# A hybrid encoder trunk on one core: setup with the modulation first, latent weights loaded raw ahead, two tiles kept on chip, and the first gate formed in the output stage

## The chip, the cores and the metric
The kernel runs on one core of a Trainium2 chip. The metric is the device time of one execution in microseconds (us). All matrix products of the model run on TensorE as three products of a high and a low part ("hi", "lo") in float32r, so that a weight or an activation is always split first: ScalarE copies the high part, VectorE or GpSimd subtracts it from the source to give the low part.

## The reference
Two layers over a sequence of 2048 tokens of width 1024. Each layer is `x + gate * RMSNorm(mixer(RMSNorm(x) * (1 + scale) + shift))`, where shift, scale and gate come from `silu(c) @ ada_w + ada_b`.
```
def _even_mixer(h, cos, sin, w_in, ...):
    rq, rk, rv, rg, cq, ckv, kr, mg = _split(h @ w_in, EV_SPLITS)
    # A: bidirectional retention on rq, rk (rope), rv, chunks of 128; * silu(rg)
    # B: latent attention: q from rmsnorm(cq) @ w_uq, k and v from rmsnorm(ckv) @ w_ukv,
    #    one rotary key kr shared by 4 heads, dense softmax; * silu(mg)
    return jnp.concatenate([ret_out, mla_out], axis=-1) @ w_out
```
The second layer's mixer (a convolution module) is not touched.

## The kernel before
The work is a row of stages. Each stage is one block with its own semaphores, in which the five engines run their own written-out queues; a stage starts when every engine has ended the one before. SP issues all loads and stores.

`setup` (L129) loads `ada_w` in eight slabs of 1024 KB and the first weight columns (`w1`, 1536 wide) in eight slabs of 768 KB, in turn. VectorE adds the slabs weighted by `silu(c)` into `acc` (L323, L326), with the rope angles (L266 to L279), the decay logarithms (L289 to L299) and exponents (L305 to L311) after the first sums. ScalarE makes `w_hi` (L205), GpSimd `w_lo` (L229). TensorE then turns `acc` into columns (L240) for `shift` and `gain`.

`project_retention` (L338) goes over 16 tiles of 128 tokens, last tile first. Per tile: norm (L454, L457), transpose (L606), modulation (L466), split (L472, L543), three projections `ps_qk`, `ps_v`, `ps_g` of 24 matmuls (L612 to L614), rope, the backward state. `h` and a pack of 2560 columns are stored for each tile (L417, L422). The gate row of the modulation is summed on the side (L578).

`project_mla` (L695) goes over the tiles forwards. Its weight pieces come through four staging slots in the two packs, four of them loaded ahead in the stage before; ScalarE and VectorE split them (L672, L680). TensorE forms the first gate (L1109, L1110), VectorE multiplies it by the post-norm weight (L1016), and only then the tiles begin: `ps_cq`, `ps_ckv`, the retention scores, `ps_mg`, and the up projections `ps_cq`, `ps_mg`, `ps_s` out of the latents (L1027 to L1029).

`attention` (L1118) loads the shared rotary key whole (L1285) and splits it in two forms `kr_same` and `kr_swap` of 2048 columns (L1344, L1462, L1466, L1468) before the first scores (L1484). `even_out` (L1552) splits the output weight in eight pieces, transposes mix tiles (L1757) and multiplies (L1779 to L1781); its residual step uses the first gate (L1734).


## Time and profile before
| what | value |
|---|---|
| time, median of 3 runs | 2511.83 us (2511.54 to 2513.14) |
| profiled execution, its own time | 2515.42 us |
| its span | 2513.6 us |
| TensorE busy | 2286.7 us, 91% |
| VectorE, ScalarE, GpSimd busy | 55%, 45%, 40% |
| mean granted clock of TensorE | 0.969 of full |

The span is the time from the first to the last instruction. Engines are named PE (TensorE), PEld (its weight loads), DVE (VectorE), ACT (ScalarE), POOL (GpSimd), SP (SyncE); a q after the name means its queue of DMA issues. [...] In brackets behind an instruction stands how long its engine sat idle before it and who released it.

### The profile page before, as it was taken

To read this page: it belongs to the slowest core of one execution; us is meant where nothing else is said; L and a number is where in the kernel's file an instruction comes from. 1 tells how busy PE (TensorE), PEld (TensorE's weight loads), DVE (VectorE), ACT (ScalarE), POOL (GpSimd) and SP (SyncE) were. 2 spreads that over 40 slices of the span, in tenths; PEclk is the share of its full clock that TensorE was granted. 3 is DMA by queue.
4 is the path that set the end of the run, shared out by engine and by line. 5 is a ranking of instruction groups with operands and counts; after the bars stand their busy time and mean duration, and the time that the engine had idled before them with its cause. 6 is when DMAs were issued, how large, how long until landed. Compare 5 with 4: busy or idle time off the path is not lost. (4 is left out here: it accounts for less than half of the span.)

```text
span 2513.6 us, 34469 instructions
## 1 busy us (share of the span) xinstructions
PE 2286.7 (91%) x11378; PEld 1898.7 (76%) x11378; DVE 1392.1 (55%) x2092; ACT 1132.4 (45%) x2090; POOL 1011.9 (40%) x741
## 2 busy tenths in 40 slices
PE   0799997999998699999999969997999999995998
PEld 0688885989887487787887758885878888874886
DVE  8233334434433577777777631114888889864332
ACT  2444443222222455555555535554455555553332
POOL 4222220222222423233233102333789998873443
PEclk9999998999999899999999979998999999997999
DMA  6234335334343533343342133321011112124553
GB/s 258 103 139 146 133 117 197 137 132 143 131 148 102 153 104 97 98 113 96 104 113 80 47 130 126 125 101 42 26 50 52 59 65 70 55 109 130 162 149 115
DMA packets 194607, 279.94 MB, mean 111 GB/s; under 512 B 10837, under 2 KB 139221, under 8 KB 189271
## 3 DMA queue, kind: packets, MB, share of 16 engines
q1 hardware_dynamic: 189910, 270.41, 33.4%
q10 hardware_dynamic: 4608, 8.39, 0.9%
q8 instruction: 51, 0.84, 0.1%
q14 instruction: 38, 0.30, 0.0%
HBM read 188.05 MB, written 90.70 MB: 111 GB/s over the span
## 5 line engine op out<-in xcount | busy, mean ns | idle before, releaser
L1957 POOL TENSOR_TENSOR conv_g<-conv_g,product 128x1024 f32<-128x1024 f32 x160 | 379.5, 2415 | 41.4 <-ACT product L1986 41.4
L2053 DVE SCALAR_TENSOR_TENSOR ps_conv<-u,cols,ps_conv 128x1024 f32<-128x1024 f32 x304 | 364.8, 1285 | 0.0
L2092 PE MATMUL ps_z<-ho_hi,wp_lo 128*128 128x512 f32 x768 | 302.6, 394 | 23.9 <-POOL wp_lo L1947 18.9
L2093 PE MATMUL ps_z<-h_left,wp_hi 128*128 128x512 f32 x768 | 301.7, 393 | 0.0
L2094 PE MATMUL ps_z<-ho_hi,wp_hi 128*128 128x512 f32 x768 | 301.4, 392 | 0.0
L1986 ACT ACTIVATE product<-u,cols 128x1024 f32<-128x1024 f32 x160 | 181.9, 1151 | 144.5 <-POOL conv_g L1957 139.1
L1315 ACT ACTIVATE pt_hi<-ps_pt 128x512 fp32r<-128x512 f32 x256 | 154.2, 603 | 200.3 <-PE ps_pt L1496 198.8
L1414 DVE TENSOR_TENSOR pt_lo<-ps_pt,pt_hi 128x512 fp32r<-128x512 f32 x256 | 176.0, 688 | 116.8 <-ACT pt_hi L1315 114.1
L1404 DVE TENSOR_REDUCE mx<-ps_s 128x1 f32<-128x512 f32 x256 | 173.4, 685 | 39.8 <-PE ps_s L1488 38.8
L2092 PEld LDWEIGHTS ps_z<-ho_hi,wp_lo 128*128 128x128 f32 x768 | 146.0, 190 | 56.2 <-POOL wp_lo L1947 19.7
L1308 ACT ACTIVATE probs<-ps_s,bias 128x512 f32<-128x512 f32 x256 | 174.0, 698 | 24.1 <-DVE bias L1410 16.5
L1360 POOL TENSOR_TENSOR v_lo<-v_st,v_hi 128x512 fp32r<-128x512 f32 x64 | 84.1, 1314 | 242.9 <-DVE v_hi L1390 242.9
L2094 PEld LDWEIGHTS ps_z<-ho_hi,wp_hi 128*128 128x128 f32 x768 | 145.9, 190 | 30.8
L2093 PEld LDWEIGHTS ps_z<-h_left,wp_hi 128*128 128x128 f32 x768 | 146.2, 190 | 30.2
L1496 PE MATMUL ps_pt<-const,probs 128*128 128x128 f32 x1024 | 154.2, 273 | 4.1 <-DVE pt_lo L1414 3.1
L1496 PEld LDWEIGHTS ps_pt<-const,probs 128*128 128x128 f32 x1024 | 125.5, 140 | 42.8 <-DVE pt_lo L1414 11.5
L1355 POOL TENSOR_TENSOR k_lo<-k_st,k_hi 128x512 fp32r<-128x512 f32 x64 | 85.8, 1353 | 169.7 <-ACT k_hi L1299 169.6
L1484 PE MATMUL ps_s<-k_hi,q_lo 128*128 128x512 f32 x256 | 114.5, 447 | 36.4 <-DVE kr_swap L1468 23.6
L1505 PE MATMUL ps_ot<-pt_hi,v_lo 128*128 128x512 f32 x256 | 111.2, 434 | 5.1 <-ACT o_t L1334 5.1
L2338 PE MATMUL ps_yo<-w_last_hi,mo_lo 128*128 128x512 f32 x256 | 103.3, 404 | 7.8 <-DVE mo_lo L2283 7.8
L1734 DVE SCALAR_TENSOR_TENSOR mod_acc<-ps_y,ry_e,gate 128x1024 f32<-128x1024 f32 x16 | 20.5, 1284 | 154.9 <-POOL ry_e L1707 154.9
L1779 PE MATMUL ps_y<-wo_hi,m_lo 128*128 128x512 f32 x256 | 103.2, 403 | 0.0
(341 smaller groups left out, 5668.7 us busy)
## 6 DMA issues: line engine op xcount, KB each, us to landing
scratch_ret_pack<-pack SPq DMA_DIRECT2D x16, 1280.0 KB, 5.4
pack<-scratch_ret_pack SPq DMA_DIRECT2D x16, 1280.0 KB, 6.7
k_st<-scratch_k_t SPq DMA_DIRECT2D x64, 256.0 KB, 3.5
v_st<-scratch_v SPq DMA_DIRECT2D x64, 256.0 KB, 3.7
ada<-in_ada_w_dram SPq DMA_DIRECT2D x16, 768.0 KB, 6.4
wp_raw<-in_od_w_in_dram SPq DMA_DIRECT2D x24, 512.0 KB, 3.9
ada<-in_ada_w_dram SPq DMA_DIRECT2D x8, 1024.0 KB, 6.3
xt<-in_x_dram SPq DMA_DIRECT2D x16, 512.0 KB, 6.2
```

The source lines that it names most:

```text
L1308: act.activation(probs[s][b][:, kb * BANK:(kb + 1) * BANK], ps_s[kb][:], ACT.Exp, bias=bias[b % 2][:], scale=SCALE, accum_out=sums[s][:, b ...
L1315: act.activation(pt_hi[kt % 4][:], ps_pt[kt % 2][:], ACT.Copy).then_inc(pthi_done, 1)
L1404: dve.tensor_reduce(mx[:, kb:kb + 1], ps_s[kb][:], AX.X, ALU.max).then_inc(max_done, 1)
L1414: dve.tensor_tensor(pt_lo[kt % 4][:], ps_pt[kt % 2][:], pt_hi[kt % 4][:].bitcast(F32), ALU.subtract).then_inc(ptlo_done, 1)
L1484: pe.matmul(dst, q_lo[s][:, q], k_hi[s][:, k], start=True, stop=False)
L1496: mm = pe.transpose(ps_pt[kt % 2][:, qb * P:(qb + 1) * P], probs[sl][qb][:, kt * P:(kt + 1) * P], ident)
L1957: pool.tensor_tensor(half(conv_g, h), half(conv_g, h), product[h][:], ALU.add).then_inc(added, 1)
L1986: act.activation(product[h][:], units(c, V_TAPS + i, h), ACT.Copy, scale=tap_w).then_inc(product_done, 1)
L2053: ins = dve.scalar_tensor_tensor(acc[h][:], units(c, k, h), w, acc[h][:], ALU.mult, ALU.add)
L2092: pe.matmul(dst, lo[:, k, :], h_hi[:, k, t], start=k == 0, stop=False)
L2093: pe.matmul(dst, hi[:, k, :], h_lo[:, k, t], start=False, stop=False)
L2094: mm = pe.matmul(dst, hi[:, k, :], h_hi[:, k, t], start=False, stop=k == KD - 1)
```

## The change
Five parts.

**Setup.** Only the two last tiles of x and `ada` are loaded at first, then `w1` raw into the place of `w_lo`, in three thirds of columns. The modulation sums are kept in PSUM (`acc_ps`), and their columns are summed after a transpose. The decay logarithms and exponents come first on VectorE. The first tile's norm and transposes, and the high part of the first weight third, are made here.
```
-            for k in range(KD + 1):
-                if k < KD:
-                    if k >= NW:
-                        sp.wait_ge(mod_sum, k - NW + 1)
-                    sp.dma_start(ada[:, k % NW, :], ada_view[k][:, 0:2 * D]).then_inc(ada_in[k % NW], 16)
-                if k > 0:
-                    n = k - 1
-                    if n >= NS:
-                        sp.wait_ge(lo_done, n - NS + 1)
-                    sp.dma_start(stage[:, n % NS, :], w_view[n][:, w_cols[0]:w_cols[1]]).then_inc(w_in[n % NS], 16)
-            for dst, src in ahead:
-                sp.dma_start(dst, src).then_inc(x_ahead, 16)
-            sp.wait_ge(x_ahead, 16 * len(ahead))
+            for i, src in enumerate(x_pieces):
+                sp.dma_start(xt[:, i, :], src).then_inc(x_ahead[i], 16)
+            for k in range(KD):
+                if k >= NW:
+                    sp.wait_ge(mod_sum, k - NW + 1)
+                sp.dma_start(ada[:, k % NW, :], ada_view[k][:, 0:2 * D]).then_inc(ada_in[k % NW], 16)
+            for j in range(3):
+                for k in range(KD // 2):
+                    sp.dma_start(w_raw[:, 2 * k:2 * k + 2, j * BANK:(j + 1) * BANK],
+                                 w_view[k][:, :, j * BANK:(j + 1) * BANK]).then_inc(w_in[j], 16)
+            sp.wait_ge(x_ahead[1], 16)
...
-            split_w(1)
-            act.wait_ge(v_step, 101)
-            act.activation(st.sin[:].rearrange("p t f -> p (t f)"), red[:, 0, :], ACT.Sin)
-            act.activation(st.cos[:].rearrange("p t f -> p (t f)"), red[:, 1, :], ACT.Sin).then_inc(a_step, 1)
-            act.wait_ge(v_step, 102)
+            act.wait_ge(v_step, 3)
             act.activation(tiny[:, 1, :], tiny[:, 0, :], ACT.Exp, scale=-1.0).then_inc(a_step, 1)
+            act.wait_ge(x_ahead[0], 16)
+            act.activation(sq, xt[:, 0, :], ACT.Square, accum_out=ssq[:]).then_inc(sq_done, 1)
+            act.wait_ge(rstd_done, 1)
+            act.activation(xn[:], xt[:, 0, :], ACT.Copy, scale=rstd[:]).then_inc(xn_done, 1)
...
+            act.wait_ge(w_in[0], 64)
+            for k in range(KD // 2):
+                at = slice(2 * k, 2 * k + 2), slice(0, BANK)
+                act.activation(w_hi[:, *at], w_raw[:, *at], ACT.Copy)
...
-            pool.memset(st.neg_half[:], -0.5)
-            for k in range(KD):
-                pool.wait_ge(hi_done, k + 1)
-                pool.tensor_tensor(w_lo[:, k, :], stage[:, k % NS, :], w_hi[:, k, :].bitcast(F32),
-                                   ALU.subtract).then_inc(lo_done, 1)
+            pool.memset(st.neg_half[:], -0.5).then_inc(ms_done, 1)
+            pool.wait_ge(sq_done, 1)
+            pool.tensor_scalar(ms[:], ssq[:], 1.0 / D, EPS, ALU.mult, ALU.add).then_inc(ms_done, 1)
+            pool.wait_ge(ms_done, 2)
+            pool.tensor_tensor(rstd[:], ms[:], st.neg_half[:, 0:1], ALU.pow).then_inc(rstd_done, 1)
...
+            pe.wait_ge(xn_done, 1)
+            for k in range(KD):
+                pe.transpose(ps_h[k // 4][:, (k % 4) * P:(k % 4 + 1) * P], xn[:, k * P:(k + 1) * P], ident)
             pe.wait_ge(mod_sum, KD)
             for m in range(2 * KD):
-                mm = pe.matmul(mod_ps[:, m:m + 1], acc[:, m * P:(m + 1) * P], ones[:, 0:1], start=True, stop=True)
-            mm.then_inc(mod_done, 1)
+                mm = pe.transpose(acc_ps[:, m * P:(m + 1) * P], acc[:, m * P:(m + 1) * P], ident)
+                if m % 4 == 3:
+                    mm.then_inc(mod_turned, 1)
...
                     dve.wait_ge(mod_sum, k)
-                    ins = dve.scalar_tensor_tensor(acc[:], ada[:, k % NW, :], st.silu_c[:, k:k + 1], acc[:], ALU.mult, ALU.add)
+                    if k == KD - 1:
+                        dve.wait_ge(sq_done, 1)
+                    ins = dve.scalar_tensor_tensor(acc if k == KD - 1 else acc_ps[:], ada[:, k % NW, :],
+                                                   st.silu_c[:, k:k + 1], acc_ps[:], ALU.mult, ALU.add)
                 ins.then_inc(mod_sum, 1)
...
-            dve.wait_ge(mod_done, 1)
+            for m in range(4):
+                dve.wait_ge(mod_turned, m + 1)
+                ins = dve.tensor_reduce(mods[:, 4 * m:4 * m + 4], acc_ps[:, m * BANK:(m + 1) * BANK].rearrange("p (a b) -> p a b", b=P),
+                                        AX.X, ALU.add)
+            step(ins)
```
**Retention stage.** The angles, sine and cosine move here, and so do the low parts of all weight thirds and the high parts of two. The latent columns of the next stage's weights (`first_raw`, 640 wide, all eight rows of blocks) are loaded raw once the waves are made. The last two tiles are not stored; their `h` and packs stay on chip.
```
             step(0, 0, 0)
+            sp.wait_ge(waves_done, 1)
+            for dst, src in ahead:
+                sp.dma_start(dst, src).then_inc(ahead_in, 16)
             step(1, 1, 0)
...
-                store(NT - 2 + s, s)
             sp.wait_ge(ahead_in, 16 * len(ahead))
             for s in range(2):
-                sp.wait_ge(h_stored[s], 16 * NT // 2)
-                sp.wait_ge(pack_stored[s], 16 * NT // 2)
+                sp.wait_ge(h_stored[s], 16 * (NT // 2 - 1))
+                sp.wait_ge(pack_stored[s], 16 * (NT // 2 - 1))
...
+            split_w(1)
             norm(1, 1, 0)
+            act.wait_ge(angles_done, 1)
+            act.activation(st.sin[:].rearrange("p t f -> p (t f)"), red[:, 0, :], ACT.Sin)
+            act.activation(st.cos[:].rearrange("p t f -> p (t f)"), red[:, 1, :], ACT.Sin).then_inc(waves_done, 1)
+            split_w(2)
             def step(t, s, pair):
                 turn_out(t + 1, 1 - s, pair + s)
...
+            pool.sem_inc(ms_ready, 1)
+            pool.sem_inc(rstd_ready, 1)
+            split_w(0)
+            split_w(1)
             rstds(1, 1)
+            split_w(2)
             for t in range(2):
                 rotate(t)
                 rstds(t + 2, t)
...
             dve.memset(back[:], 0.0).then_inc(back_copied, 1)
             dve.wait_ge(back_copied, 1)
+            split_w(0)
+            angles()
             split_lo(0, 0)
+            residues()
+            split_w(1)
+            split_w(2)
...
+                if isinstance(t, int) and t == 0:
+                    pe.wait_ge(wlo_done[0], 4)
...
+                if isinstance(t, int) and t == 0:
+                    pe.wait_ge(wlo_done[1], 4)
                 project(ps_v, s, BANK, v_done)
...
+                if isinstance(t, int) and t == 0:
+                    pe.wait_ge(wlo_done[2], 4)
                 project(ps_g, s, 2 * BANK, g_done)
```
**Second projection stage.** Tiles 0 and 1 use what lies on chip. Latent weights are split at once; the other columns and the up-projection weights are loaded raw into the place of their low parts and split by pieces, the latter inside tile 0. The gate is no longer formed here.
```
-            load_h(0)
-            sp.dma_start(gate_bias, st.rows[:, R_GATE:R_GATE + D]).then_inc(row_in, 16)
-            sp.dma_start(post, st.rows[:, R_POST:R_POST + D].broadcast_to([P, D])).then_inc(post_in, 16)
-            load_pieces(sp, pieces, stage, w_in_sem, wlo_done, AHEAD)
-            sp.wait_ge(wlo_done, NP)
-            load_pack(0, 0)
+            for k in range(KD // 2):
+                sp.dma_start(wi_raw[:, 2 * k:2 * k + 2, LORA:], tail_view[k][:, :, RET_COLS + LORA:RET_COLS + MLA_COLS])\
+                  .then_inc(tail_in[k], 16)
+            sp.dma_start(ukv_raw[:], ukv_view).then_inc(ukv_in, 16)
+            sp.dma_start(uq_raw[:], uq_view).then_inc(uq_in, 16)
...
+                if isinstance(t, int) and t == 0:
+                    split_up()
...
-                if not (isinstance(t, int) and t == NT - 1):
+                if not (isinstance(t, int) and t in (0, NT - 1)):
                     split_h(t + 1, 1 - s)
...
+            act.sem_inc(hi_ready, 2)
+            for k in range(KD):
+                act.activation(wi_hi[:, k, 0:LORA], first_raw[:, k, :], ACT.Copy).then_inc(lora_hi, 1)
+            for k in range(KD // 2):
+                act.wait_ge(tail_in[k], 16)
+                at = slice(2 * k, 2 * k + 2), slice(LORA, MLA_COLS)
+                act.activation(wi_hi[:, *at], wi_raw[:, *at], ACT.Copy).then_inc(tail_hi, 1)
...
+            for k in range(KD // 4):
+                at = slice(2 * k, 2 * k + 2), slice(MG, MLA_COLS)
+                pool.wait_ge(tail_hi, k + 1)
+                pool.tensor_tensor(wi_lo[:, *at], wi_raw[:, *at], wi_hi[:, *at].bitcast(F32), ALU.subtract).then_inc(mg_lo, 1)
...
-                hold(dve, st, pack_in[s], 16 * pair + 16)
+                if not (isinstance(t, int) and t < 2):
+                    hold(dve, st, pack_in[s], 16 * pair)
...
+                if isinstance(t, int) and t == 0:
+                    split_up()
                 hold(dve, st, chi_ready, t + 1)
...
+            dve.sem_inc(lo_ready, 2)
+            for k in range(KD):
+                dve.wait_ge(lora_hi, k + 1)
+                dve.tensor_tensor(wi_lo[:, k, 0:LORA], first_raw[:, k, :], wi_hi[:, k, 0:LORA].bitcast(F32),
+                                  ALU.subtract).then_inc(lora_lo, 1)
+            for k in range(KD // 2):
+                at = slice(2 * k, 2 * k + 2), slice(LORA, MG)
+                dve.wait_ge(tail_hi, k + 1)
+                dve.tensor_tensor(wi_lo[:, *at], wi_raw[:, *at], wi_hi[:, *at].bitcast(F32), ALU.subtract).then_inc(kr_lo, 1)
+            for k in range(KD // 4, KD // 2):
+                at = slice(2 * k, 2 * k + 2), slice(MG, MLA_COLS)
+                dve.tensor_tensor(wi_lo[:, *at], wi_raw[:, *at], wi_hi[:, *at].bitcast(F32), ALU.subtract).then_inc(mg_lo, 1)
...
+                first = isinstance(t, int) and t == 0
+                in_columns(ps_cq, s, 0, QR, cq_done, lora_lo if first else None)
                 pe.wait_ge(v_out, t)
+                if first:
+                    pe.wait_ge(kr_lo, KD // 2)
                 in_columns(ps_ckv, s, CKV, KVR + ROPE, ckv_done)
...
+                if first:
+                    pe.wait_ge(mg_lo, KD // 2)
                 in_columns(ps_mg, s, MG, H * DV, mg_done)
...
-                pe.wait_ge(wlo_done, NP)
+                if first:
+                    pe.wait_ge(up_lo, (KVR + QR) // P)
...
-            pe.wait_ge(row_in, 16)
-            for n in range(2):
-                c = slice(n * BANK, (n + 1) * BANK)
-                pe.matmul(gate_ps[n][:], ones, st.gate[0][:, c], start=True, stop=False)
-                mm = pe.matmul(gate_ps[n][:], ones[0:1, :], gate_bias[:, c], start=False, stop=True)
-            mm.then_inc(gate_step, 1)
-            pe.wait_ge(gate_step, 2)
-            pe.wait_ge(wlo_done, KD)
```
**Attention.** The rotary key is loaded by ScalarE's queue in parts of 512 and 1536 columns; the first query's low part is made by VectorE, not GpSimd.
```
 
-            for half in range(2):
-
-                sp.dma_start(probs[0][0][half * ROPE:(half + 1) * ROPE, :], st.kr_t).then_inc(kr_in, 16)
+            load_k(0, 0)
             load_q(0)
...
-            act.activation(kr_same[:], probs[0][0][:], ACT.Copy).then_inc(kr_hi, 1)
-            for q in range(QB):
+            for i, c in enumerate(KR_PARTS):
+                for half in range(2):
+                    r = slice(half * ROPE, (half + 1) * ROPE)
+                    act.dma_start(probs[0][0][r, c], st.kr_t[:, c]).then_inc(kr_in[i], 16)
+            for i, c in enumerate(KR_PARTS):
+                act.wait_ge(kr_in[i], 32)
+                act.activation(kr_same[:, c], probs[0][0][:, c], ACT.Copy).then_inc(kr_hi, 1)
+                act.activation(kr_swap[:, c], probs[0][0][:, c], ACT.Copy).then_inc(kr_hi, 1)
+                if i == 0:
+                    split_k(0, 0, 0)
+            for q in range(1, QB):
                 split_k(0, 0, q)
-            act.wait_ge(kr_ready, 2)
+            act.wait_ge(kr_ready, 4)
             over_groups(act, group)
...
-            split_q(0, 0)
+            pool.sem_inc(q_ready, 1)
...
 
-            dve.wait_ge(kr_in, 32)
-            dve.tensor_copy(kr_swap[:], probs[0][0][:]).then_inc(kr_hi, 1)
             split_q(0, 0)
-            dve.wait_ge(kr_hi, 2)
-
-            dve.tensor_tensor(kr_same[ROPE:P, :], probs[0][0][ROPE:P, :], kr_same[ROPE:P, :].bitcast(F32),
-                              ALU.subtract).then_inc(kr_ready, 1)
-            dve.tensor_tensor(kr_swap[0:ROPE, :], probs[0][0][0:ROPE, :], kr_swap[0:ROPE, :].bitcast(F32),
-                              ALU.subtract).then_inc(kr_ready, 1)
+            dve.wait_ge(qhi_done, 1)
+            dve.tensor_tensor(q_lo[0][:], q_st[:], q_hi[0][:].bitcast(F32), ALU.subtract).then_inc(qlo_first, 1)
+            for i, c in enumerate(KR_PARTS):
+                dve.wait_ge(kr_hi, 2 * i + 2)
+                dve.tensor_tensor(kr_same[ROPE:P, c], probs[0][0][ROPE:P, c], kr_same[ROPE:P, c].bitcast(F32),
+                                  ALU.subtract).then_inc(kr_ready, 1)
+                dve.tensor_tensor(kr_swap[0:ROPE, c], probs[0][0][0:ROPE, c], kr_swap[0:ROPE, c].bitcast(F32),
+                                  ALU.subtract).then_inc(kr_ready, 1)
             over_groups(dve, group)
 
         @block.tensor
...
+                if isinstance(n, int) and n == 0 and b == 0:
+                    pe.wait_ge(qlo_first, 1)
+                    pe.wait_ge(kr_ready, 2 if kb == 0 else 4)
```
**Output stage.** It forms the first gate before its first tile.
```
-            sp.dma_start(gate_bias[:], st.rows[:, R_GATE + D:R_GATE + 2 * D]).then_inc(row_in, 16)
+            sp.dma_start(gate_bias[:, 0], st.rows[:, R_GATE:R_GATE + D]).then_inc(row0_in, 16)
+            sp.dma_start(post[:], st.rows[:, R_POST:R_POST + D].broadcast_to([P, D])).then_inc(row0_in, 16)
...
+            dve.wait_ge(gate0_done, 1)
+            dve.wait_ge(row0_in, 32)
+            dve.tensor_tensor(st.gate[0][:], ps_y[1][:], post[:], ALU.mult).then_inc(gate0_ready, 1)
+            dve.wait_ge(gate0_ready, 1)
...
+                if isinstance(t, int) and t == 1:
+                    pe.wait_ge(gate0_ready, 1)
...
+            pe.wait_ge(row0_in, 32)
+            for n in range(2):
+                c = slice(n * BANK, (n + 1) * BANK)
+                pe.matmul(ps_y[1][:, c], ones, st.gate[0][:, c], start=True, stop=False)
+                mm = pe.matmul(ps_y[1][:, c], ones[0:1, :], gate_bias[:, 0, c], start=False, stop=True)
+            mm.then_inc(gate0_done, 1)
```

## Rows read from the trace of the kernel before
**Rows 1.** Waits of TensorE over the span: us in total, times, longest.
```profile
PE mod_ps L240 <- DVE acc L326: 60.5, 1, 60.5
PE ps_s L1484 <- DVE kr_swap L1468: 23.6, 1, 23.6
...
PE ps_m L1757 <- DVE wo_lo L680: 13.6, 1, 13.6
```
**Rows 2.** Timeline of the setup: start us, duration us, engine, line, operation.
```profile
11.66 0.69 DVE L266 TENSOR_TENSOR ang<-pos,table 128x512 f32<-128x512 f32 x1
...
15.42 3.42 POOL L229 TENSOR_TENSOR w_lo<-stage,w_hi 128x1536 fp32r<-128x1536 f32 x1 [14.58 <-ACT w_hi L205]
...
15.50 4.42 DVE L276 SCALAR_TENSOR_TENSOR red<-turns,red 128x1024 f32<-128x1024 f32 x1
...
25.68 2.35 DVE L326 SCALAR_TENSOR_TENSOR acc<-ada,silu_c,acc 128x2048 f32<-128x2048 f32 x1
...
28.29 0.17 DVE L289 TENSOR_SCALAR tiny<-tiny 128x8 f32<-128x8 f32 x1 [0.26 <-ACT tiny L215]
...
32.40 0.17 DVE L299 TENSOR_TENSOR lg<-turns,tiny 128x8 f32<-128x8 f32 x1
...
38.10 0.17 DVE L311 TENSOR_SCALAR expw<-lg 128x8 f32<-128x8 f32 x1
...
74.27 1.98 SPq L425 DMA_DIRECT2D pack<-in_ev_w_in_dram  x4
```
**Rows 3.** The page's groups: VectorE's convolution steps.
```profile
L2053 DVE SCALAR_TENSOR_TENSOR ps_conv<-u,cols,ps_conv 128x1024 f32<-128x1024 f32 x304 | 364.8, 1285 | 0.0
```
**Rows 4.** Windows, all engines: busy us of PE, PEld, DVE, ACT, POOL; PEclk; DMA.
```profile
12.00:16.00 4.00, 0.00 (x0) 0.00 (x0) 3.79 (x7) 1.48 (x1) 0.58 (x1) 1.00 1.01 423
...
818.00:820.00 2.00, 0.00 (x0) 0.00 (x0) 0.00 (x0) 0.00 (x0) 0.00 (x0) 0.50 0.96 209
...
1486.00:1488.00 2.00, 0.00 (x0) 0.00 (x0) 1.66 (x2) 0.91 (x1) 0.00 (x0) 0.50 0.34 137
```
**Rows 5.** Timeline of the retention stage's head.
```profile
77.59 1.97 PE L606 MATMUL ps_h<-const,xn 128*128 128x128 f32 x8 [4.60 <-ACT xn L457]
...
79.60 2.91 ACT L466 ACTIVATE ht<-ps_h,shift,gain 128x128 f32<-128x128 f32 x8 [2.06 <-PE ps_h L606]
...
82.54 1.06 ACT L472 ACTIVATE h_hi<-ht 128x1024 fp32r<-128x1024 f32 x1
...
83.71 1.23 DVE L543 TENSOR_TENSOR h_lo<-ht,h_hi 128x1024 fp32r<-128x1024 f32 x1 [8.77 <-ACT h_hi L472]
...
84.98 0.80 PE L612 MATMUL ps_qk<-w_hi,h_lo 128*128 128x512 f32 x1 [5.42 <-DVE h_lo L543]
...
92.73 1.03 PE L606 MATMUL ps_h<-const,xn 128*128 128x128 f32 x8
```
**Rows 6.** Timeline from the retention stage into the second projection stage.
```profile
399.22 0.33 SPq L422 DMA_DIRECT2D scratch_ret_pack<-pack  x1
...
404.77 0.34 SPq L826 DMA_DIRECT2D ht<-scratch_h_t  x1
...
408.15 2.08 PE L1109 MATMUL ps_cq<-gate,const 128*128 128x512 f32 x2 [9.74 <-DMA turned<-in_rows_dram]
...
420.99 0.69 PE L1027 MATMUL ps_cq<-wi_hi,h_lo 128*128 128x384 f32 x1 [4.76 <-DVE gate L1016]
...
443.12 0.50 PE L1027 MATMUL ps_cq<-ukv_hi,ct_lo 128*128 128x512 f32 x1
```
**Rows 7.** Timeline of attention's head.
```profile
825.00 3.36 DVE L1466 TENSOR_TENSOR kr_same<-probs,kr_same 64x2048 fp32r<-64x2048 f32 x1
...
831.68 0.80 PE L1484 MATMUL ps_s<-k_hi,q_lo 128*128 128x512 f32 x1 [23.63 <-DVE kr_swap L1468]
```
**Rows 8.** Timeline of the output stage's head, TensorE.
```profile
1488.23 1.97 PE L1757 MATMUL ps_m<-const,mix_e 128*128 128x128 f32 x8 [13.61 <-DVE wo_lo L680]
```
**Rows 9.** Windows, TensorE alone: busy us (instructions), PEclk, DMA share, GB/s.
```profile
412.00:416.00 4.00, 4.00 (x5) 0.50 0.99 380
```

More of the change, by code:

```diff
@@ L126, in open_store, with setup @@
     return st
-def setup(nc, st, const, cols, row, positions, ada_w, layer, w, w_cols, w_hi, w_lo, ahead):
+def setup(nc, st, const, cols, row, positions, pos, ada_w, layer, w, w_hi, w_raw, w_in, xt, x_pieces, xn, ps_h, spare):
     with ExitStack() as ctx:
@@ new lines, in hybrid_trunk @@
+        project_retention(nc, st, x, xt, xn, ps_h, w_hi, w_lo, w_raw, w_in, pos, turning, h_hi, h_lo, pack, ahead, ada_w[0])
+        weights.close()
+        back_in_raw = (in_raw("ct_hi", 0, [P, 5 * P], F32R), in_raw("ct_lo", 5 * P, [P, 5 * P], F32R),
+                       in_raw("kn", 10 * P, [P, H * NOPE]), in_raw("qn", 14 * P, [P, H * NOPE]),
+                       [in_raw(f"turned{i}", (18 + 11 * i) * P, [P, 11 * P]) for i in range(2)])
+        project_mla(nc, st, ev_w_in, ev_w_uq, ev_w_ukv, first_raw, h_hi[::-1], h_lo[::-1], pack[::-1], back_in_raw)
```

349 lines of the change are left out of this document (206 added, 143 removed).

## The prediction
> **What bounds the kernel now.** I read the page first: TensorE is busy 91% of 2513.6 us. So only two things count: TensorE's idle stretches, and stretches in which it runs slow. The view of waits lists them [rows 1]. The largest is 60.5 us before the first modulation matmuls, then 23.6 us before attention's scores and 13.6 us before the first tile of the output stage. Then I read the timelines of the five places the diff touches. [...] L326 takes 2.35 us alone. But L276, 1,024 columns wide, takes 4.42 us when it starts 0.08 us behind a 3.42 us GpSimd instruction: it waits for that to end and then needs 1.1 us [rows 2]. Inside tiles of both projection stages TensorE waits for almost nothing, so a gain at a stage's head is kept, and a gain inside helps nothing.
>
> **Setup.** Removed: GpSimd's `w_lo` work (to the next stage), the angle chain, the pairing of `ada` and weight transfers. The new VectorE chain: inputs at 4.9, logit and three small steps to about 6.2, the table load and Exp of 1.5 us, then the log chain, 4.3 us from 28.29 to its end after 32.40 [rows 2]; that gives 12.1. The exponents are eight steps at about 0.35 us each plus three small ones, 3.4 us (from the end of the third sum at 34.9 to 38.3 [rows 2]): 15.5. Eight sums follow, now accumulated in PSUM. The row with both a PSUM source and a PSUM result is L2053: 1.285 us for 1,024 columns, so about 2.4 us for 2,048 [rows 3]; against 2.35 us from SBUF [rows 2] this is no loss. Eight at 2.45 us with their semaphores, and 0.6 us for the decay folds, end at 35.7. Is the data there? The DMA engines moved 423 GB/s [rows 4]; 0.5 MB small inputs, 1 MB of x and 8.4 MB of `ada` are in by about 28.5, so VectorE decides. Sixteen transposes at 0.25 us (eight took 1.97 [rows 5]) give 39.7, the last reduction and three small steps 41.1. Beside that, ScalarE's `w_hi` for the first 512 columns needs 2.1 MB more, in by 33.6 at 423 GB/s, plus 4.2 us: 38 to 39, hidden. At the 209 GB/s of attention's loads of 2 to 8 KB rows [rows 4] it would be 43: then 2 us. The next stage starts 0.9 us later: 42.0 in place of 74.27 [rows 2].
>
> **Head of the retention stage.** Before: 10.7 us from 74.27 to the first matmul at 84.98 [rows 2, 5]. Now the norm and transposes are done, but four moved pieces stand before VectorE's `h_lo`: two `w_lo` pieces (1.23 us each), six angle steps (3.8 us, 11.66 to 15.50 [rows 2]) and `h_lo` (1.23 us), 7.5 us, and 8.0 with the memset of 0.5. GpSimd holds four pieces of 1,024 columns, 2.3 us each by L229's 3.42 us for 1,536. If the two engines exclude each other for whole instructions, as L276 shows, the chain is 8.0 + 9.2 us, so the first matmul is at 59.4; if they overlapped fully, 50.4. I take 59.4: the row is unambiguous, and all four GpSimd pieces become ready within that time (ScalarE has turned, copied and split at 46.3 by 2.91 and 1.06 [rows 5], the second column third's first pieces at 47.4).
> [...]
> Later needs in tile 0: the second weight third is split at 65.8 and asked for at 68.5, the last at 73.9 and asked for at 73.9 (qk takes 7.8 us, from 84.98 to 92.73 [rows 5], v's 24 matmuls 5.6). Sine, cosine and their table load sit ahead of the last third on ScalarE; VectorE's rope waits for them. I count 0.5 us of stall. Saved at the start: 84.98 - 59.4 - 0.5 = **25**; from both sides 20 (three microseconds each for slower weight data and for stalls) to 33.
>
> **Projection to projection.** Before: the last retention store is issued at 399.22 and the next stage starts at 404.77, because SP waits for the landing; VectorE's last step ends some 1.1 us after the issue. With the last two tiles kept on chip that wait goes: start at 401.2. Then no h load and no gate matmuls: one ScalarE and one VectorE piece of 640 columns (0.75 and 0.8 us) and TensorE starts at 402.8, against 420.99 [rows 6]. But it outruns its supply. The latent columns go at VectorE's pace and the low clock, to 410; the tail of 2.4 MB is in at 409, split at 411.5; ckv to 415 to 417.5; the up projections wait for `split_up`, which stands in ScalarE's and VectorE's queues ahead of the gate activation and of `ct_hi`: 5.1 us there, so ready at 426 to 429.5, against 443.12 [rows 6]. Saved: **15.5**, from 13.5 to 17.5. Not 18, since the queues give 2.5 back.
>
> **Attention's head.** The scores start at 831.68, after two kr subtractions, the first of 3.36 us, in VectorE's queue [rows 7]. Pieces let the first key block start at about 825, but the other three need the second piece: VectorE's 64x1536 steps (1.75 us each alone) meet GpSimd's `k_lo` again, and q's low part has moved onto VectorE. I get 831.3 for block two and the same end within 1.2 us. Transfers are the same 2.6 MB on busy engines, so four more issues from ScalarE move only their order. Saved: **1**, from -1 (every step waits for GpSimd) to +4 (none does).
>
> **Output stage.** Here the change costs. TensorE stands 13.6 us, to 1488.23, waiting for weights [rows 8]. The new gate matmuls stand in its queue before that wait but need the `post` row, issued after all weight pieces and the second mix tile. The transfers fall to 137 GB/s in 1486 to 1488 [rows 4], so it lands at about 1486.7. The four matmuls took 8.1 us (2.08 for the first [rows 6]); behind them wait the transposes of mix tile 1 and tile 0. Start 1494.9 instead of 1488.23: **-6.5**. The bounds: -8.5 if `post` lands at 1489, and -4 if they run at the full clock. The granted clock stayed 0.50 in 412 to 416, with TensorE busy all of it [rows 9], so I take 8.1. Tile 0 then starts at the low clock as before.
> [...]
> The gate multiply (1.3 us) on VectorE is hidden beside tile 0's 12 us; tile 1 waits for it only in name.
>
> **Sum.** 25 + 15.5 + 1 - 6.5 = 35. It is made against the profiled execution, 2513.6 us of span and 2515.4 us of time; its time is 0.14% over the median of 2511.8, so I subtract from the median: **2476.8 us**. Measurement tells about 0.2% (5 us) from no change.
>
> **Rivals.**
> 1. The two engines overlap more than L276 shows: first matmul at 50 to 55, 5 to 8 us more: 2470. For it: 4.42 us is one pair of instructions, and VectorE may win its turn more often. Against: nothing in that pair overlaps. Chance 0.12.
> 2. [...] Chance 0.08.
> 3. Supply takes the place of the setup: weight thirds arrive or are split late, each tile-0 phase waits 3 to 4 us and the clock falls in between. 10 to 12 us given back: 2488. For it: the last third has no slack. Chance 0.18.
> 4. Slower than before. One mechanism: the first tiles of the retention stage stay at the low clock because waits on the split weights keep breaking TensorE's work. A tile has 72 matmuls at 0.43 instead of 0.235 us, 14 us a tile; more than two and a half such tiles eat the 35. At four tiles: 2533. Against it: all thirds are split once, by 74. Chance 0.02.
> 5. The change does not do what it says: setup still ends near 70, because PSUM accumulation or the data costs 5 us a sum instead of 2.4: 2500. Chance 0.04.
> The forecast itself: 0.56, its own range 2472 to 2482.
> Range: all but rival 5, rival 4 and the far end of 3: **2465 to 2488**. Faster 0.96, within 0.2% 0.02, slower 0.02.
>
> **What would show it.** In the new profile: the retention stage's first matmul at 57 to 61 and the setup's last VectorE step near 41; L229's successors of 2.3 us with VectorE steps stretched beside them; TensorE resuming 4 to 5 us after the last retention tile; the first up projection 25 to 28 us after the stage's start; a stretch of 8 us of gate matmuls at 0.50 just ahead of the output stage's tile 0, tile 0 starting some 6.5 us later after that stage's start than before. The prediction is wrong if the retention stage's first tile lasts over 25 us, if the first matmul is later than 63, or if the tiles after the second differ in length from before.

## The result, and the profile after

The changed kernel takes **2488.3 us** (median of 4 runs, 2486.7 to 2490.1) against 2512.5 us for the kernel before (4 runs on the same chip): ratio 0.9904, 95% interval 0.9886 to 0.9921. It is faster by 24.2 us. Forecast were 35 us, with a range that ended at 2488.0. So the sign was right, and the time lies just outside the range.

The page of the changed kernel, parts 1 and 3; the last row is the queue that brings instructions:

```profile
PE 2283.5 (92%) x11362; PEld 1896.5 (76%) x11362; DVE 1388.0 (56%) x2107; ACT 1133.0 (46%) x2100; POOL 996.4 (40%) x740
...
q14 instruction: 57, 0.47, 0.1%
```

Its view of waits, TensorE:

```profile
PE ps_s L1577 <- DVE kr_swap L1558: 23.8, 2, 21.8
PE acc_ps L238 <- DVE pack L309: 21.7, 1, 21.7
...
PE ps_qk L665 <- DVE h_lo L556: 18.1, 1, 18.1
...
PE ps_pt L1589 <- DVE pt_lo L1504: 12.3, 12, 3.0
PE ps_y L1927 <- DMA post<-in_rows_dram: 11.8, 1, 11.8
```

Beside [rows 1] the 60.5 us before the modulation are down to 21.7 us, with 18.1 us more before the first retention tile; the wait of attention's head is all but unchanged at 23.8. New is the wait for the `post` row, which was forecast. The wait for `pt_lo` was 3.1 us in the kernel before and is 12.3 us now, which was not forecast.

The way to see where 24 us came from is to take the same event in both traces and follow how far the changed kernel is ahead. All times are starts in the two profiled executions (spans 2513.6 and 2487.0 us, 26.6 us apart). The row of `ps_turn` is the last but one of attention's sixteen; the last one follows 18.1 us later in both:

| event | before | after | ahead by | in this stretch | forecast |
|---|---|---|---|---|---|
| first retention matmul | 84.98 | 55.68 | 29.3 | +29.3 | +25 |
| `ps_qf` of the last retention tile | 396.48 | 362.02 | 34.5 | +5.2 | 0 |
| last `ps_tr` of the latent projection | 807.77 | 759.17 | 48.6 | +14.1 | +15.5 |
| first `ps_pt` of attention | 869.54 | 824.33 | 45.2 | -3.4 | +1 |
| last but one `ps_turn` of attention | 1442.48 | 1411.02 | 31.5 | **-13.7** | 0 |
| tile 0 of the output stage | 1489.85 | 1464.64 | 25.2 | -6.3 | -6.5 |
| last matmul | 2503.68 | 2477.03 | 26.7 | +1.4 | 0 |

One stretch decides: 13.7 us are lost between the first and the last group of attention, where no line of VectorE's loop was changed. The prediction has no term there.

**Start.** Setup and the head of the retention stage, by the timeline:

```profile
31.64 2.35 DVE L309 SCALAR_TENSOR_TENSOR pack<-ada,silu_c,acc_ps 128x2048 f32<-128x2048 f32 x1
38.62 0.17 DVE L320 SCALAR_TENSOR_TENSOR gain<-scale,cols 128x8 f32<-128x8 f32 x1
39.76 11.68 POOL L532 TENSOR_TENSOR w_lo<-w_raw,w_hi 128x1024 fp32r<-128x1024 f32 x4 [30.62 <-POOLq L74]
40.28 6.20 DVE L613 TENSOR_TENSOR w_lo<-w_raw,w_hi 128x1024 fp32r<-128x1024 f32 x2
46.40 2.84 DVE L593 TENSOR_TENSOR ang<-pos,table 128x512 f32<-128x512 f32 x1
54.40 1.23 DVE L556 TENSOR_TENSOR h_lo<-ht,h_hi 128x1024 fp32r<-128x1024 f32 x1
55.68 0.80 PE L665 MATMUL ps_qk<-w_hi,h_lo 128*128 128x512 f32 x1 [18.11 <-DVE h_lo L556]
```

The last sum takes 2.35 us with PSUM as its second source, and the six before it, with a PSUM result too, take 14.64 us, 2.44 each: as sized. Two `w_lo` pieces take 6.20 us beside GpSimd's, and 2.35 us later in the trace, without them: the exclusion of [rows 2] is there again. GpSimd's four pieces take 11.68 us, about four times 2.3 and two VectorE pieces of 1.23.

**Between the projections.** TensorE starts again 4.7 us after it last worked on the last retention tile, and the first up projection comes 27.4 us after the stage's first instruction (366.80):

```profile
368.63 0.66 PE L1108 MATMUL ps_cq<-wi_hi,h_lo 128*128 128x384 f32 x1 [4.67 <-DVE wi_lo L1089]
...
394.22 0.50 PE L1108 MATMUL ps_cq<-ukv_hi,ct_lo 128*128 128x512 f32 x1 [1.47 <-DVE ct_lo L1036]
```

**Attention's head.** The first scores start 1.8 us nearer to the stage's beginning, but then TensorE stands. The first row of each fence is VectorE's copy of the query's rotary part, in the kernel before and in the changed one. It comes 15.8 us after the last `ps_tr` there and 18.3 us after it here, because its load lands later:

```profile
823.60 0.43 DVE L1396 CAST q_rot<-qr_st 128x512 fp32r<-128x512 f32 x1 [0.66 <-DMA qr_st<-scratch_qr_t]
```

```profile
777.43 0.43 DVE L1486 CAST q_rot<-qr_st 128x512 fp32r<-128x512 f32 x1 [19.07 <-DMA qr_st<-scratch_qr_t]
...
781.29 0.77 PE L1577 MATMUL ps_s<-k_hi,q_lo 128*128 128x512 f32 x1 [21.85 <-DVE kr_swap L1558]
...
781.43 6.55 POOL L1445 TENSOR_TENSOR k_lo<-k_st,k_hi 128x512 fp32r<-128x512 f32 x3 [5.86 <-ACT k_hi L1381]
...
782.89 2.71 DVE L1558 TENSOR_TENSOR kr_swap<-probs,kr_swap 64x1536 fp32r<-64x1536 f32 x1
...
785.75 0.77 PE L1577 MATMUL ps_s<-k_hi,q_lo 128*128 128x512 f32 x1 [1.99 <-DVE kr_swap L1558]
```

**Attention's loop.** VectorE's timeline, the first steps after three of the gaps:

```profile
1086.19 0.69 DVE L1504 TENSOR_TENSOR pt_lo<-ps_pt,pt_hi 128x512 fp32r<-128x512 f32 x1 [4.52 <-issue]
...
1166.15 0.69 DVE L1504 TENSOR_TENSOR pt_lo<-ps_pt,pt_hi 128x512 fp32r<-128x512 f32 x1 [5.08 <-issue]
...
1247.09 0.69 DVE L1504 TENSOR_TENSOR pt_lo<-ps_pt,pt_hi 128x512 fp32r<-128x512 f32 x1 [4.51 <-issue]
```

"issue" means that nothing in the profile held the engine. The loop makes four passes of two groups each, 76.6 us a pass in the kernel before. The three gaps shown, of 4.52, 5.08 and 4.51 us, lie 80 and 81 us apart, one in each of the last three passes; the first pass has one of 3.71 us before 1006.83, which the view puts down to `pt_hi`. Measured from `ps_turn` to `ps_turn`, a group lasts 38.2 to 38.4 us in the kernel before, the last two apart. After, one group in each of the four passes lasts 40.2, 41.0, 43.2 and 42.6 us (from the `ps_turn` at 983.93 to the one at 1024.15, 1062.52 to 1103.51, 1141.89 to 1185.08, 1223.43 to 1265.99): 1.9, 2.7, 4.9 and 4.3 us over 38.3, together 13.8, which is the loss in the table. The instruction queue brought 57 packets instead of 38 (0.47 MB: 8.2 KB each), and the surplus of 19 falls into these passes. From 1000 to 1320 us, where the four long groups lie, it brought 20, five in each 80 us:

```profile
q14 instruction: 20, 0.16, 0.2%
```

In the kernel before, the same view of 1030 to 1350 us has no row for this queue.

**Output stage.** The forecast, line by line; the last row is the window of the gate matmuls, with TensorE busy for 7.99 of 8 us at a granted clock of 0.50 of full:

```profile
1455.01 2.08 PE L1927 MATMUL ps_y<-gate,const 128*128 128x512 f32 x2 [11.85 <-DMA post<-in_rows_dram]
1457.01 2.07 PE L1928 MATMUL ps_y<-gate_bias,const 1*128 1x512 f32 x2
...
1464.64 0.78 PE L1912 MATMUL ps_y<-wo_hi,m_lo 128*128 128x512 f32 x1
...
1455.00:1463.00 8.00, 7.99 (x8) 0.50 0.56 204
```

### The profile page after: what moved, and what is told of

The parts are those of the page before. It is cut to its first block and busy times, and to the rows that moved or that the text cites. A ratio compares the mean times of both kernels' runs of the same rounds, so it can differ in the third digit from the quotient of the medians.

```text
span 2487.0 us, 34444 instructions
## 1 busy us (share of the span) xinstructions
PE 2283.5 (92%) x11362; PEld 1896.5 (76%) x11362; DVE 1388.0 (56%) x2107; ACT 1133.0 (46%) x2100; POOL 996.4 (40%) x740
## 5 line engine op out<-in xcount | busy, mean ns | idle before, releaser
L2231 PE MATMUL ps_z<-ho_hi,wp_lo 128*128 128x512 f32 x768 | 301.4, 393 | 24.1 <-POOL wp_lo L2086 18.9
L1589 PE MATMUL ps_pt<-const,probs 128*128 128x128 f32 x1024 | 154.7, 274 | 13.6 <-DVE pt_lo L1504 12.3
L1577 PE MATMUL ps_s<-k_hi,q_lo 128*128 128x512 f32 x256 | 116.3, 454 | 36.6 <-DVE kr_swap L1558 23.8
```

Source lines behind the costliest of these rows:

```text
L1589: mm = pe.transpose(ps_pt[kt % 2][:, qb * P:(qb + 1) * P], probs[sl][qb][:, kt * P:(kt + 1) * P], ident)
L2231: pe.matmul(dst, lo[:, k, :], h_hi[:, k, t], start=k == 0, stop=False)
```

## The experiments

These are sixteen runs of fifteen kernels (`b_hfront` ran twice). Profile figures are from one profiled execution each; times are medians, with the ratio to the kernel before on the same chip.

### Instruction fetch: a_pad40, a_pad14, b_pad20

In the built program attention's loop has 293 VectorE instructions. It begins at VectorE's instruction 670 before and 684 after. These three move it, and nothing else:

```
+            for _ in range(40):          # 14 in a_pad14; 20 in b_pad20, on the kernel before
+                dve.sem_inc(st.held, 1)
             split_q(0, 0)
```

> The changed kernel with 40 more VectorE instructions (increments of a semaphore that nobody waits on) ahead of attention's loop, where VectorE waits for the first loads anyway. In the changed kernel four iterations' second halves lasted 1.9, 2.7, 4.9 and 4.3 us over the usual 38.3 us, and VectorE stood 4.5 to 5.1 us on nothing but issue before a pt_lo step; the instruction queue q14 brought 57 packets of 8.2 KB against 38 in the kernel before, all of the surplus inside that loop. Theory A (the loop's 293 VectorE instructions, which start 14 instructions later than before, now lie so that a part of them is fetched anew in each iteration): 40 more move the loop clear of that place; no issue idle before pt_lo, q14 back to about 38 packets, 13.8 us gained: 2474.5 us (2472 to 2477). Theory B (the long groups come from something else, such as where buffers lie or how transfers collide): no change, 2488.3 us within 2 us, 57 packets. [...]

> The same with 14 more instead of 40: the control. [...] The kernel before (loop at VectorE instruction 670) had no stall and the one after (at 684) had it, so 14 further on (698) it must still have it: 2488.3 us within 2 us, 55 to 58 packets. Theory B: no change either. A third possibility, that any added instruction there cures it: 2474.5.

> The kernel before with 20 such instructions at the same place, so that its loop starts at VectorE instruction 690. Theory A: it gets the stall: four groups long by 2 to 5 us, q14 55 to 58 packets in place of 38, 10 to 15 us slower, 2512.5 + 13.8 = 2526.3 us. Theory B: 2512.5 within 2 us, 38 packets.

| | loop starts at | q14 packets | extra time of the four passes | time | ratio |
|---|---|---|---|---|---|
| before | 670 | 38 | none | | 1 |
| after | 684 | 57 | 1.9, 2.7, 4.9, 4.3 | 2488.3 | 0.9904 |
| b_pad20 | 690 | 57 | 2.3, 4.5, 2.8, 1.2 | 2522.6 | 1.0038 (1.0025 to 1.0052) |
| a_pad14 | 698 | 58 | 0.7, 1.0, 3.9, 0.9 | 2479.7 | 0.9870 (0.9855 to 0.9885) |
| a_pad40 | 724 | 38 | none | 2475.6 | 0.9848 (0.9834 to 0.9861) |

The queue's row in a_pad40 and in b_pad20:

```profile
q14 instruction: 38, 0.31, 0.0%
```

```profile
q14 instruction: 57, 0.47, 0.1%
```

Theory A holds, in both directions. 40 instructions that do nothing take the changed kernel from a ratio of 0.9904 to 0.9848, 14 us by the ratios (12.7 by the medians, on two chips); 20 make the kernel before slower by 10.7 us, and its four passes are longer by the same 10.8 us. The control a_pad14 fetches anew as well, as forecast (that 14 more instructions had to leave the fetches in place was the author's estimate), but that cost 6.6 us instead of 13.8, so its time was missed by 8.6 us. In these kernels, whether the loop fetches goes with where it begins. How much that costs is not fixed by it: a_rows_first, below, has the same start of 684 and loses 10.5 us. What sets the cost stays open. The longest of VectorE's gaps on nothing but "issue" in this loop is 5.08 us. That a fetch is what VectorE stands for is inferred: the surplus packets and the long groups come and go together in these five kernels, and no row shows the one holding up the other.

### Output stage: a_rows_first

```
+            sp.dma_start(gate_bias[:, 0], ...).then_inc(row0_in, 16)
+            sp.dma_start(post[:], ...).then_inc(row0_in, 16)
             load_mix(0, 0)
             load_pieces(sp, pieces, stage, w_in, wlo_done)
             load_mix(1, 1)
-            (the same two transfers)
```

> The changed kernel with the two row transfers for the first gate (gate_bias, post) issued first of all in the output stage instead of behind the mix and weight pieces. Theory (the prediction's step for the output stage: 8.1 us of gate matmuls stand behind the post row and ahead of tile 0): they now run while TensorE waits for weights anyway, so tile 0 starts within 1 us of the split of the last weight piece: 6 us gained, 2482.3 us (2481 to 2484), and the wait of ps_y for DMA post (11.8 us) falls under 2 us. Rival: the rows take the place of the first weight pieces, which then land 1.5 to 2 us later: 2484 to 2485. Rival: the wait for weights simply takes over whole, no gain: 2488.

```profile
1441.69 2.07 PE L1928 MATMUL ps_y<-gate_bias,const 1*128 1x512 f32 x2
1449.37 1.97 PE L1888 MATMUL ps_m<-const,mix_e 128*128 128x128 f32 x8 [5.61 <-DVE wo_lo L1669]
1450.99 0.78 PE L1912 MATMUL ps_y<-wo_hi,m_lo 128*128 128x512 f32 x1
```

Measured 2479.5 us (0.9876, 0.9861 to 0.9891). Tile 0 starts 47.1 us after attention's last but one `ps_turn`, against 53.6 in the changed kernel and 47.4 before: 6.5 us come back, and TensorE waits for the weights alone. The profiled span fell by 11.2 us to 2475.8. Only 6.5 of it is the repair: 3.3 us are the loop, whose fetches (57 packets) cost 10.5 us here instead of 13.8, another 3.6 us are attention's head, and the stretch after tile 0 takes 2.5 us more. The time was forecast at 2482.3, so this run was 2.8 better than its theory, for reasons outside it.

### Head of the retention stage: c_hlo_first

```
             split_w(0)
+            split_lo(0, 0)
+            split_w(1)
+            split_w(2)
             angles()
-            split_lo(0, 0)
             residues()
-            split_w(1)
-            split_w(2)
```

ScalarE's `split_w(2)` moves ahead of `norm(1, 1, 0)` as well; the 40 instructions of a_pad40 are in.

> The changed kernel with the 40 VectorE instructions (2475.5 us) and another order at the head of the retention stage: VectorE makes the first h_lo right after its two first weight pieces, then the other weight pieces, and only then the angles; ScalarE splits the last weight third before the sine and cosine. h_lo stood at 54.4 us behind 8 us of angle steps, while h_hi was ready at 43.8 and the last w_lo piece of VectorE's at 46.4. Theory D (VectorE's queue order sets the start; beside GpSimd each of its steps takes 1.2 to 3.1 us): h_lo ends at 48 to 49, first retention matmul at 49.5 in place of 55.7, all of it kept if the rope of tile 0 ends by 68: 2469.3 us (2468 to 2471). Rival: the angles now end at 65 to 67, the rope comes late, and TensorE waits for it before tile 1: 2 to 5 us given back, 2472 to 2474. Rival: GpSimd's four pieces hold VectorE off until 51.4, and h_lo comes at 52 to 53: 2 us gained, 2473.5.

```profile
68.48 0.63 ACT L488 ACTIVATE sin<-red 128x512 f32<-128x512 f32 x1 [11.25 <-DVE red L606]
...
70.38 0.68 DVE L567 TENSOR_TENSOR rs<-ps_qk,sin 128x512 f32<-128x512 f32 x1
...
72.79 1.04 POOL L521 TENSOR_TENSOR qf<-qk,q_w 128x512 f32<-128x512 f32 x1
...
73.88 1.12 PE L691 MATMUL ps_qf<-const,qf 128*128 128x128 f32 x4 [4.17 <-POOL qf L521]
...
68.00:78.00 10.00, 5.82 (x25) 0.68 0.00 1
```

The last row is TensorE's window from 68 to 78, with the granted clock behind the busy time. The same window in a_pad40:

```profile
68.00:78.00 10.00, 10.00 (x54) 1.00 0.01 2
```

The first matmul is at 49.92, 5.9 us earlier, so theory D is right as to the start. But the time is 2476.7 (0.9861, 0.9846 to 0.9876) against 0.9848: nothing is gained. TensorE waits 4.2 us for `qf` at the end of tile 0, because the angles, now last, delay the rope. That is the first rival, at a higher price than its 2 to 5 us: the granted clock from 68 to 78 is 0.68, where a_pad40 has 1.00, and at the last retention tile the kernel is 1.2 us behind a_pad40, so 7.1 us were given back.

### Attention's head: c_head_old

`attention` as in the kernel before, with the 40 instructions.

> The changed kernel, still with the 40 VectorE instructions ahead of attention's loop (2475.5 us, the comparison here), with attention's head as in the kernel before: rope keys loaded whole by SyncE first of all, no pieces, q's low part on GpSimd. In the changed kernel the head came out worse than forecast: its first scores start 22.4 us after the last turn of the projection stage (24.1 before), but VectorE's q copies start 18.5 us after it instead of 16.1, the second key block waits for kr_swap's second piece until 785.7, and the first value block starts 3.4 us further from the last turn than before (65.4 against 62.0). Theory C (the four extra issues from ScalarE put the rope keys and q behind each other, and the stop between the first and the second key block keeps TensorE at the low clock): undoing the head gives 3.4 us back, 2472 us (2471 to 2473.5). Rival: the loss comes from the transfers of the stage before, which end closer to the head, and stays: 2475.5. Rival from the prediction (the pieces gain 1): 2476.5.

Measured 2471.8 us, 0.9846 (0.9833 to 0.9860), on another chip than a_pad40 with its 0.9848: by the ratios no difference that these runs can tell. The profiles do show one. From the last `ps_tr` to the first `ps_pt` the seven profiles with the split head take 61.6 to 65.2 us (mean 63.7), and the eleven with the whole load 60.4 to 61.8 us (mean 61.3), all runs of this document taken together. So the pieces cost about 2 us instead of saving 1.

Two things add up to it. First, the early start is eaten. TensorE starts 1.5 to 4 us earlier and then stands 2 to 3.5 us after one key block. VectorE's query copies come 16.0 to 18.3 us after the last `ps_tr`, where the whole load has 15.3 to 15.8, and the second key block starts after 25.1 to 26.6 us; the forecast had it at 23.5 (831.3 less 807.8). The second block of queries then starts after 33.0 to 35.0 us, against 31.8 to 33.2 with the whole load. Second, the clock comes late: the windows of the changed kernel against the kernel before (second fence), each for the first and the second block of queries:

```profile
786.00:793.00 7.00, 6.16 (x15) 0.60 0.61 170
793.00:801.00 8.00, 6.44 (x20) 0.79 0.88 270
```

```profile
833.00:840.00 7.00, 6.00 (x18) 0.71 0.66 171
840.00:847.00 7.00, 4.83 (x20) 1.00 0.97 299
```

The fourth column is the granted clock. The second block takes 8.4 us at 0.79 to 0.80 in six of the seven profiles with pieces. In a_rows_first it has 1.00 and takes 6.8, and there nothing is lost, although its stop of 3.5 us is the longest. So the late clock costs 1.6 us where it occurs; that the stop brings it is argued, not shown.

### Where h lies: b_hfront, b_shift64, b_h32, d_h0

Retention tiles 1 to 15 take 291.6 us before and 286.3 after. The matmuls of 512 columns are the same, but follow each other after 0.2343 and 0.2290 us. b_hfront allocates `h_hi` and `h_lo` ahead of the weights, as the change does; the others put 32 to 96 bytes in front of an operand.

```
+        h_hi = [weights.enter_context(nc.sbuf_tensor(f"h_hi{i}", ...)) for i in range(2)]
+        h_lo = [weights.enter_context(nc.sbuf_tensor(f"h_lo{i}", ...)) for i in range(2)]
         w_hi, w_lo = ...
```

> The kernel before with h_hi and h_lo of the retention stage placed in front of the weights, as in the changed kernel (their address then is 32 over a multiple of 128 bytes instead of 0; the weights stay at 32 over). In the retention stage the matmuls of 512 columns follow each other after 0.2343 us before and 0.2295 us after, 19.50 and 19.15 us a tile, which gives 5 us over the stage that no step of the prediction had. Theory E (where the stationary h tiles lie decides): 0.2295 us here, 5 us faster, 2507. Rival F (where the moving weights lie decides, 96 over instead of 32 over): 0.2343, 2512. Rival G (it is the other work beside it, the smaller transfers and stores): 0.2343, 2512.

> The kernel before with 64 bytes left free in front of the first weights, so that they lie 96 bytes over a multiple of 128, as in the changed kernel, and h 64 over. Rival F: 0.2295 us from matmul to matmul in the retention stage, 5 us faster, 2507. Theory E: 0.2343 or another value, since h lies otherwise again. Rival G: 0.2343, 2512.

> The kernel before with 32 bytes left free in front of h_hi in the retention stage, so that h_hi and h_lo start 32 bytes over a multiple of 128 instead of 0, in the same region; the weights do not move. With both moved to the front the spacing of the 512-column matmuls fell and the tiles after the first took 284.5 us instead of 291.6. Theory E1 (the 32 bytes over a multiple of 128 decide): 284 to 287 us here too, 5 to 7 us faster. Theory E2 (the region decides: h in front of the weights, or its distance from them): 291.6, no gain.

> The changed kernel with the 40 VectorE instructions, its h_hi and h_lo moved by 96 bytes to a multiple of 128, all else left where it was within 128. Theory E1: retention tiles as slow as in the kernel before, 0.2343 us from matmul to matmul, 5 us slower, 2480. Theory E2: 0.2295 us as in the changed kernel, 2475.5.

### The same, continued: b_hfront_timed, b_hfront0, e_w32, e_h64

> The kernel before with h_hi and h_lo in front of the weights, timed. One profile of it showed 0.2275 us from matmul to matmul in the retention stage against 0.2343, 7.1 us less for the tiles after the first, and one time of 2502.7 us. If placement alone does this: 7 to 8 us faster than the kernel before, ratio 0.997. If the single time was chance: a ratio of 1.000.

> As b_hfront, but 96 bytes further, so that h starts on a multiple of 128 bytes, and 32 more ahead of the weights, which stay 32 over. Spacings so far with the weights 32 over: h behind them at 0: 0.2343; behind at 32: 0.2323; in front at 32: 0.2275. Theory E1 (offset within 128 decides, the region adds little): 0.234 here. Theory E2 (region decides): 0.2275 to 0.229.

> The kernel with all three repairs (2465 us) and 64 bytes left free ahead of the first weights, so that they lie 32 over a multiple of 128, h in front at 32. If offsets of both operands decide, this is the pairing of b_hfront: 0.2275 us instead of 0.2290, 1.6 us over the stage, 2463.3 us. If it is the distance between them instead: any value from 0.2275 to 0.2343.

> The kernel with all three repairs, h 64 over a multiple of 128 instead of 32, the weights 96 over as they were. In the kernel before, h at 64 over (behind the weights, these 96 over) gave 0.2339. If 0 and 64 are the slow offsets: 0.234, 5 us slower, 2470. If only 0 is: 0.229, 2465.

| kernel | h, bytes over 128 | weights | h stands | matmul to matmul | tiles 1 to 15 | time |
|---|---|---|---|---|---|---|
| before | 0 | 32 | behind | 0.2343 | 291.6 | |
| b_shift64 | 64 | 96 | behind | 0.2339 | 291.6 | 2508.8, one |
| b_h32 | 32 | 32 | behind | 0.2323 | 289.8 | 2506.1, one |
| b_hfront, then _timed | 32 | 32 | in front | 0.2275 | 284.5 | 2502.7, one; 2504.0, ratio 0.9972 (0.9962 to 0.9982) |
| b_hfront0 | 0 | 32 | in front | 0.2334 | 290.7 | 2512.8, one |
| after | 32 | 96 | in front | 0.2290 | 286.3 | |
| d_h0 | 0 | 96 | in front | 0.2338 | 291.1 | 2484.2, one |
| e_w32 | 32 | 32 | in front | 0.2323 | 289.6 | 2468.0 |
| e_h64 | 64 | 96 | in front | 0.2342 | 291.8 | 2474.8, one |

Four matmuls in a row in b_hfront_timed, 0.68 us from the first start to the fourth; at 0.2343 it would be 0.70, so single rows hardly show what the mean over the stage does:

```profile
250.27 0.39 PE L611 MATMUL ps_g<-w_lo,h_hi 128*128 128x512 f32 x1
250.49 0.39 PE L612 MATMUL ps_g<-w_hi,h_hi 128*128 128x512 f32 x1
250.72 0.39 PE L610 MATMUL ps_g<-w_hi,h_lo 128*128 128x512 f32 x1
250.95 0.39 PE L611 MATMUL ps_g<-w_lo,h_hi 128*128 128x512 f32 x1
```

Placement is shown: h put in front of the weights, which moves these by 16 KB at the same offset, makes the kernel before 7 us faster, 32 bytes in front of h alone (b_h32) shorten its tiles by 1.8 us, and h moved back to 0 in the changed kernel (d_h0) takes 4.8 us of the retention tiles away again. Every kernel with h on an offset of 0 or 64 is at 0.2334 to 0.2343; only with 32 was it faster. The first of these comparisons puts rival G (other work beside it) out, and b_shift64, with the weights at 96 and no gain, puts rival F out. But 32 does not fix the value (0.2275, 0.2290, 0.2323 twice). b_h32 took 289.8 us, between the 284 to 287 of theory E1 and the 291.6 of E2, and e_w32 missed: with b_hfront's two offsets it was slower than without its gap, though h had not moved. One rival is not tested. The weights lay at 32 or 96 in every kernel, so h at 32 always means as well that h and the weights lie a multiple of 64 bytes apart; the runs cannot tell h's own offset from this distance. What else of the addresses counts stays open.

### The repairs together: d_both, d_all

d_both is a_pad40 with a_rows_first; d_all has attention's old head as well.

> The changed kernel with the 40 VectorE instructions and with the gate's rows issued first in the output stage. If the two causes add (13.8 us of fetches in attention's loop, 6.5 us of late gate rows): 2488.3 - 13 - 6.5 = 2469 us (2467 to 2471), 38 packets on the instruction queue, tile 0 of the output stage 47 us after the last turn of attention (53.6 in the changed kernel). Rival: they overlap, since the loop's end moves where the rows are loaded: 2472 to 2475.

> The same with attention's head as in the kernel before. Theory C: in five profiles with the split head the first value block starts 61.6 to 65.2 us after the last turn of the projection stage (mean 63.5), in five with the whole load 60.4 to 61.8 (mean 61.3); so 2 us less, 2467 us, and 61 to 62 here. Rival (the split head is worth what the prediction gave it, or nothing): 2469 to 2470.

| | time | ratio to before |
|---|---|---|
| d_both | 2465.0 (2464.8 to 2470.0) | 0.9822 (0.9809 to 0.9835) |
| d_all | 2464.9 (2462.9 to 2468.5) | 0.9819 (0.9806 to 0.9833) |

The causes add: from 0.9904 to 0.9822 is 20.6 us, where 14 and 6.5 were found one by one. d_both was forecast at 2467 to 2471 and came out 2 us below that. Both beat both kernels. Between the two the times show nothing, while the head takes 63.9 us in the profile of the one and 61.5 in the other.

## Why the prediction was right or wrong

**What failed: the sum has no term for VectorE's instructions themselves.** The prediction read "the five places the diff touches", and attention's loop, which is none of them, was costed at nothing. But the change made VectorE's code ahead of it 14 instructions longer, and from there each pass of the loop fetches instructions again: 13.7 us in the profile. Without it (a_pad40) the kernel takes 2475.6 us, 1.2 us from the forecast of 2476.8 and inside its own range of 2472 to 2482 (by the ratio it saves 38 us, where 35 were forecast). That closeness is partly luck: by the table the other terms add up to 40.3 us, with the start and the tiles 9.5 over the forecast and attention's head 4.4 under it.

**Start of the retention stage: right mechanism, 4.3 us too small.** 29.3 instead of 25. The setup's last step ends at 38.8 (41 forecast), the next stage starts at 39.7 (42.0), and from there to the first matmul it takes 16.0 us (17.4). The matmul's place, 55.7, does not decide between exclusion (57 to 61 forecast) and rival 1 (50 to 55), since it lies between them. The durations do: full overlap would take 8.4 us from the stage's start, and two VectorE pieces took 6.20 us beside GpSimd's instead of 2.35. So exclusion was the right reading of 4.42 us. The stall in tile 0 (0.5 forecast, rival 3 up to 12 us) did not come: there is no such wait. c_hlo_first shows that order is near its limit: 6 us earlier at the start come back as a wait for the rope.

**Retention tiles: +5.2, not forecast.** The text named a different tile length as a sign that it is wrong. It was one, and the runs trace it to where the operands lie, `h_hi` and `h_lo` above all. The edit looks like bookkeeping, and I costed it at nothing.

**Projection to projection: right.** 14.1 instead of 15.5, with TensorE back after 4.7 us (4 to 5 forecast) and the first up projection after 27.4 (25 to 28).

**Attention's head: wrong sign.** -3.4 in that profile, about -2 over the profiles, instead of +1; outside the bounds of -1 to +4. The step that failed is the start of the second key block, forecast 23.5 us after the last `ps_tr` and measured at 26.6: the text let the four issues from ScalarE move "only their order", but the query copies came 2.5 us later than before. Undoing the head brings them back (15.6 us in c_head_old); whether the rope keys on ScalarE's queue or the first key block ahead of the query delayed them is not separated. The text also did not ask what a late clock costs: 1.6 us in the second block of queries, in six of seven profiles. The head in the kernel before starts later and once.

**Output stage: right.** -6.3 instead of -6.5, four gate matmuls of 8.0 us at a granted clock of 0.50 throughout, and a_rows_first gives 6.5 back by the order of two transfers. So rival 2, a higher clock from midway on, is out. The 0.2 us are luck in part: from the last but one `ps_turn` to tile 0 the seven profiles built on the kernel before take 45.1 to 47.4 us, and this pair used the longest; measured against all seven, the loss is 6.2 to 8.5 us. The forecast had the repair in hand, since it says that the row is "issued after all weight pieces and the second mix tile".

**The list of waits.** The prediction names 60.5, 23.6 and 13.6 us as the largest waits of TensorE. Two of 18.9 and 17.9 us stand between them, in the second layer, which the change does not touch; the sum does not suffer from it.

## What to carry to other kernels

Before you forecast, list what a change moves without editing it: the start of each later loop in each engine's instruction stream, and the address of each matmul operand. Here the first cost 13.7 us and the second gave 5.2 us, as much as steps that were edited. After the run, compare the two traces event by event; a stretch without an edit that loses time, with "issue" ahead of an engine's steps (up to 5.08 us here) and more packets on the instruction queue (57 against 38), can be a loop that fetches anew, and idle instructions ahead of it test that in one run (40 cured it here, 14 did not). And a head that starts early only to stop again can cost more than one that starts late: here 63.7 us against 61.3 from the last `ps_tr` to the first `ps_pt`.

## What the runs showed of the hardware

A VectorE loop of 293 instructions ran without extra packets on the instruction queue where it began at instructions 670 and 724 (38 packets), and with them at 684, 690 and 698 (57 or 58), at 0.7 to 4.9 us a pass. The spacing of 512-column matmuls at full granted clock varied from 0.2275 to 0.2343 us with the placement of their operands, 3% in a stage bound by TensorE; moving `h_hi` and `h_lo` made the whole kernel before 0.28% faster. Two VectorE subtractions of 128x1024 took 6.20 us beside GpSimd's and 2.35 us without them. Four float32 matmuls in a row kept TensorE busy for 8.0 us at a granted clock of 0.50.
